# Two transformer blocks on one Trainium2 core: the first memory attention's values in PSUM banks 2 and 3, and the second memory's norm turn behind them

## What is computed

```python
# first block, memory attention: 4 heads of 128
q = rmsnorm(heads(rmsnorm(x, norm_xq) @ w_mq, 4), mq_norm)
k, v = split(rmsnorm(mem, norm_mem) @ w_mkv, 2)
k = rmsnorm(heads(k, 4), mk_norm)
p = softmax(q k^T * 128**-0.5)
x = x + (p v) @ w_mo
# second block, much later; depends on mem_2 alone, so its keys are worked on early
kv = rmsnorm(mem_2, mem_g_2) @ xa_wkv_2
```

## Time and profile before

| | |
|---|---|
| median of three runs | 1182.5 us (1180.4 to 1182.51) |
| profiled execution, first to last instruction | 1180.3 us |
| mean granted clock of PE in it | 0.996 |
| PE busy | 1152.7 us, 98% of the span |
| DVE busy | 811.4 us, 69% |
| ACT busy | 621.6 us, 53% |
| DMA, share of 16 engines | 49% for the weights' queue |

### The profile page before, as it was taken

One profiled execution on the slowest core, in us unless ns is written; L12 is line 12 of the kernel. 1 busy time (PEld: TensorE's weight loads), 2 busy tenths in 40 slices (PEclk: granted clock), 3 DMA queues, 4 the chain that ended last, 5 costly groups with the idle time before them and its releaser, 6 DMA issues.

```text
span 1180.3 us, 16847 instructions
## 1 busy us (share of the span) xinstructions
PE 1152.7 (98%) x6797; PEld 1006.6 (85%) x6797; DVE 811.4 (69%) x881; ACT 621.6 (53%) x801; POOL 87.0 (7%) x118
## 2 busy tenths in 40 slices
PE   8999999999999999999999999999999998999997
PEld 8978998888987799999888888888777887888886
DVE  6897657755878667878547777637866747777743
ACT  7666354435668556656436444436355546444432
POOL 7101101210000000000000000002700000000000
PEclk9999999999999999999999999999999999999999
DMA  8654323333665355555665556555634523665560
GB/s 257 195 160 150 111 82 107 112 103 108 214 214 179 107 170 170 166 192 185 211 204 177 183 183 201 192 182 169 211 111 149 187 93 123 198 212 178 179 213 36
DMA packets 144420, 193.95 MB, mean 164 GB/s; under 512 B 6168, under 2 KB 121240, under 8 KB 144344
## 3 DMA queue, kind: packets, MB, share of 16 engines
q1 hardware_dynamic: 143144, 188.43, 49.0%
q0 software_dynamic: 1200, 4.46, 1.1%
HBM read 191.82 MB, written 1.05 MB: 163 GB/s over the span
## 4 chain that ended last, share of the span: by engine, by line
PE 68%; DVE 8%; ACT 4%; issue 2%; DVEq 0%; ACTq 0%
PE banks L1371 19%; PE banks L1337 19%; PE banks L1319 10%; PE banks L1340 9%; DVE wlo L1925 3%; PE banks L1356 2%; PE banks L1347 1%; PE banks L1594 1%; ACT whi L1654 1%; PE banks L1385 1%; PE banks L1552 1%; PE banks L1473 1%; PE banks L1482 0%; DVE x_tok L2195 0%; PE banks L1549 0%
## 5 line engine op out<-in xcount | busy, mean ns | idle before, releaser
L1925 DVE TENSOR_TENSOR wlo<-raw,whi 128x2048 fp32r<-128x2048 f32 (+1 forms) x178 | 406.2, 2290 | 121.6 <-ACT whi L1654 121.3
L1654 ACT ACTIVATE whi<-raw 128x2048 fp32r<-128x2048 f32 (+1 forms) x179 | 340.0, 1903 | 239.8 <-PE banks L1340 137.9
L1337 PE MATMUL banks<-xhl,whi 128*128 128x512 f32 x1232 | 396.5, 403 | 2.7 <-DVE y5l L2250 1.8
L1340 PEld LDWEIGHTS banks<-xhl,wlo 128*128 128x128 f32 x1232 | 231.7, 188 | 54.2
L1340 PE MATMUL banks<-xhl,wlo 128*128 128x256 f32 x1232 | 242.9, 278 | 0.0
L1337 PEld LDWEIGHTS banks<-xhl,whi 128*128 128x128 f32 x1232 | 188.8, 189 | 9.6 <-issue 5.1
L1319 PE MATMUL banks<-xhl,whi 128*128 128x256 f32 x912 | 165.5, 285 | 1.2 <-DVE xhl L1952 0.7
L1319 PEld LDWEIGHTS banks<-xhl,whi 128*128 128x128 f32 x912 | 142.1, 192 | 2.1 <-DVE xhl L1952 1.1
L1319 PE MATMUL banks<-xhl,wlo 128*128 128x256 f32 x456 | 129.2, 283 | 0.0
L1371 PE MATMUL banks<-whi,hh 128*128 128x512 f32 x264 | 103.0, 390 | 0.0
L1371 PE MATMUL banks<-wlo,hh 128*128 128x512 f32 x264 | 102.9, 390 | 0.0
(11 more groups left out here) (370 smaller groups left out, 1549.0 us busy)
## 6 DMA issues: line engine op xcount, KB each, us to landing
raw<-in_w_in SPq DMA_DIRECT2D x40, 1024.0 KB, 5.3
raw<-in_w_up SPq DMA_DIRECT2D x22, 1024.0 KB, 5.6
raw<-in_ffn_w_gate SPq DMA_DIRECT2D x22, 1024.0 KB, 5.3
raw<-in_ffn_w_up SPq DMA_DIRECT2D x22, 1024.0 KB, 5.3
raw<-in_ffn_w_down SPq DMA_DIRECT2D x22, 1024.0 KB, 5.0
raw<-in_w_down SPq DMA_DIRECT2D x11, 1024.0 KB, 6.5
raw<-in_w_out SPq DMA_DIRECT2D x8, 1024.0 KB, 5.1
raw<-in_xa_wkv SPq DMA_DIRECT2D x8, 1024.0 KB, 5.3
```

Source lines behind the costliest of these rows:

```text
L1337: pe.matmul(bank(b[m]), wh[:, k, m * P:(m + 1) * P], both[:, k, :, :].rearrange("p a t -> p (a t)"), start=(k == 0), stop=(k == KD - 1), s ...
L1340: ins = pe.matmul(bank(b[m])[:, 0:T], wl[:, k, m * P:(m + 1) * P], Xh[:, k, :], start=False, stop=(k == KD - 1), skip_group_check=True)
L1654: act.activation(columns(whi, c, part), columns(raw, c, part), ACT.Copy).then_inc(act_done, 1)
L1925: dve.tensor_tensor(columns(wlo, c, part), columns(raw, c, part), columns(whi, c, part), ALU.subtract).then_inc(dve_done, 1)
```

## The change

The values' two chunks accumulate in banks 2 and 3 instead of 6 and 7. With that, the scores of head 1 no longer wait for ACT's copy of the values, in the plan and in the code. And the second memory's norm turn is no link of a chain any more: it stands in the plan behind the two chunks of values, before the two of `xk`.

```diff
@@ build_chunks
-    vals("w_mkv", 512, "m1", "vcopy", (6, 7), to="mv")
+    vals("w_mkv", 512, "m1", "vcopy", (2, 3), to="mv")
@@ input_of
-        if name == "sc" and args == ["mem", 1]:
-            return pl.ended.get(("copy", max(c for c, ch in enumerate(chunks) if ch.get("to") == "mv")), 1e9)
@@ build_plan
     side.append(hn("mq0", "mq1"))
-    turn_m2 = [[lambda: norm_turn("mem_g_2", 0, "m2")]]
-    side.append(turn_m2)
-    finished[id(turn_m2)] = max(pl.ended["nd", "mem_g_2", 1], pl.ended["add", c - 1])
     for lane in range(2):
         side.append(heads_of("mem", [lane, lane + 2]))
     mm(c)
     mm(c + 1)
     c += 2
-    while turn_m2:
-        place(turn_m2.pop(0)[0])
+    norm_turn("mem_g_2", 0, "m2")
     mm(c)
     mm(c + 1)
@@ sc, on PE
                 elif kind == "mem":
                     pe.wait_ge(dve_done, at("hn_mul", f"mq{h // 2}"))
-                    if h == 1:
-                        pe.wait_ge(act_done, at("copy", chunk_of("mv", None)))
```

## The result

The changed kernel takes 1185.71 us (median of 7 runs, 1184.9 to 1186.16) against 1182.5 for the kernel before (7 runs, 1180.4 to 1183.24). The ratio is 1.0032, with a 95% interval of 1.0023 to 1.0042. The forecast was 1185.0 us, a loss just beyond 0.2%.

What follows compares the result with a forecast made beforehand. PE, busy 1152.7 of 1180.3 us, was taken as the bound. Waits 5.55 + 0.6 - 1.05 - 2.55 and clock 1.4 - 1.4 gave about +2.5 us, so a median of 1185.0 us, range 1182 to some 1187.4.

Steps and rivals of the forecast that it cites:

- The order: PE, ACT and DVE queues from chunk 48 to 51: scores and exponentials of heads 0 and 1 precede the turn's high parts.
- the planned margin of 0.28: At chunk 48's end: the scores of heads 0 and 1 clear their hook by 0.28 of planned time, preceding the turn.
- the tie of 409.30 against 409.30: At the hook after half of chunk 50: lane 1 gets in with planned 409.30 against a limit of 409.30.
- the second rival: Before `w_mo`: head 1's output falls behind `lo` 52 on DVE, about 1.1 us more wait, 1186.1 us; chance 0.1.
- The turn's wait: Before chunk 49: its first matmul waits for the whole turn, leaving PE without work for 5.55 us.
- What is removed: `mq1`'s sum waiting on `mq0` (1.05 us), the wait before `w_mo` (2.55), the slow clock after it (1.4); together 5.0 us.
- The small wait: Before `w_mo`: chunk 51 waits for banks 0 and 1, emptied by chunk 50's `add`; 0.6 us, between 0 and 0.6.
- The clock behind chunk 49: Behind chunk 49's start: PE's slow level after the long wait costs 1.4 us, with bounds of 0 and 2.0.
- The sum: Whole kernel: waits 5.55 + 0.6 - 1.05 - 2.55 = +2.55, clock 1.4 - 1.4 = 0, so about +2.5 us.
- The first (no slow clock): Behind chunk 49's wait: no slow clock, or less of the small wait; +0.5, thus 1183 to 1184 us; chance 0.25.
- The third (turn ahead of the softmax): On ACT and DVE: turn precedes softmax, chunk 49 starts at 388.1, -2.5, thus 1180.0 us; chance 0.15 with all else faster.
- The range: Kernel time from 1182 to some 1187.4 us, leaving out the faster rival.

Runs made afterwards that it cites:

- the exchange: Against the changed kernel: banks of the second memory's two key chunks exchanged, chunk 49 in 0 and 1, chunk 50 in 2 and 3; 1182.57 us.
- the seventh kernel: Against the exchange: exponentials of heads 0 and 1 moved behind the turn's high part 3 on ACT, their maxima behind low part 7 on DVE; 1183.29 us.
- the kernel with the turn elsewhere: Against the kernel before: values in banks 2 and 3, turn still under chunk 48 but through 6, 7, 0, 1, key chunks' banks exchanged; 1179.31 us.
- The filler: Against the changed kernel: 40 transposes of the identity into unused bank 5, between the turn and chunk 49's waits; 1183.3 us.
- only the turn behind: Against the kernel before: only the turn moved behind the values, which stay in banks 6 and 7, with head 1's wait left in; 1190.09 us.
- the filler on top of the bank exchange: Against the exchange: 28 transposes of the identity added between the turn and chunk 49; 1182.42 us.

## Why the prediction came out right

- **The order.** PE, ACT and DVE run in the order that was derived; each row above falls in its place. The scores were let in, as the planned margin of 0.28 said, and so was head 1's product at the tie of 409.30 against 409.30, so the second rival did not come.
- **The turn's wait.** Predicted: PE out of work at 385.4, chunk 49 at 390.95, 5.55 us. Measured: 384.06 + 1.67 = 385.7 and 391.19, 5.5 us. Its two causes are shown one at a time: the banks by the exchange (5.2 to 3.5 us), the softmax ahead of the turn on ACT and DVE by the seventh kernel (3.5 to 1.7).
- **What is removed.** The waits of 1.05 and 2.55 us and the slow clock behind the second are gone from the changed kernel. That clock was priced a little low, at 1.4 us, because the count stopped at 409.61. In the kernel before the next matmul of `w_mo` follows only 0.61 us later; in the kernel with the turn elsewhere, in the same place behind a product, it follows after 0.42:

```profile
410.22 0.39 PE L1371 MATMUL banks<-wlo,y2h 128*128 128x512 f32 x1
```

```profile
407.70 0.58 PE L1371 MATMUL banks<-whi,y2h 128*128 128x512 f32 x1
408.12 0.39 PE L1371 MATMUL banks<-wlo,y2h 128*128 128x512 f32 x1
```

So the clock cost 1.6 us, and 5.2 us went in all. The kernel with the turn elsewhere bears it out for the two at `w_mo`: 2.55 + 1.6 = 4.15 us, and its stretch is 4.2 us shorter.
- **The small wait.** 0.6 us predicted; PE could have started `w_mo` at 411.15 + 0.44 = 411.6 and started at 411.94: 0.35.
- **The clock behind chunk 49: the term that was mis-sized.** It stood in the sum as 1.4 us, from the kernel before, with an upper bound of 2.0. From 391.19 to 396.45 PE did one quarter of chunk 49 (1.4 us at full clock, 388.40 to 389.79 in the kernel with the turn elsewhere), a sum (0.85) and four matmuls (0.7), 2.95 and 0.1 of start, in 5.26: 2.2 us. The filler gives 2.25 from outside. By the windows the slow level lay over PE's work from chunk 49's start to about 395.9; these are 4.7 us of dense matmuls, and half of that is 2.35. So the term was about 0.8 too small, and its bound, drawn from 3.6 us of slow work, too low.
- **The sum.** 5.5 + 0.35 + 2.2 - 5.2 = +2.85 against +2.55; the stretch shows 2.8, the spans 3.0, the medians 3.2. That the forecast came within 0.3 us of the stretch is in part luck: the clock behind chunk 49 was 0.8 too small, while 0.2 too little was taken off for the clock at `w_mo`, and the two waits together were put 0.3 too long.
- **The rivals.** The first (no slow clock) fails by the windows, in the one execution that was profiled. The third (turn ahead of the softmax) did not happen, and made real it was not faster either: its forecast of 1180.0 was wrong by almost 5 us, because the later softmax returns as a wait ahead of `w_mo`. The prediction priced that rival without following DVE to the end.
- **The range.** By its own words (1186.7 and a microsecond of spread) its upper end is 1187.7 and not 1187.4. Nothing hangs on it.
- **The rule.** "Perfetto Trace Analysis", section "Matmuls", in the Trainium skill, asks that independent groups of matmuls rotate through PSUM banks. The runs agree as far as the rule reaches: the exchange, which gives chunk 49 banks that the turn leaves earlier, is worth 2.8 us of the stretch, and sending the turn through the idle 6 and 7 makes the fastest kernel here. But chunk 49 is not independent of the turn, whose output it reads, and 3.5 us of its wait stayed with the exchange.

Two things are left open. Whether the last wait, 0.9 us of the sum of `mq1` for `hn_mul` of `mq0`, can go as well without a new one was not tried in the kernel with the turn elsewhere. And each size of the slow clock is that of one execution; how it spreads over executions at this place is not measured.

## What to carry to other kernels

Freeing a lane from a wait by moving an accumulation to other banks has a second half: what used those banks so far must go somewhere, and if it goes behind the accumulation it loses the matmuls that hid it. Look first for banks that the change itself makes idle (here 6 and 7, for the turn), and give the next accumulation the banks that are released first. When work is reordered, walk every engine's queue to the next point where PE waits; three of the reorderings here only moved the wait.

## What the runs showed of the hardware

A wait of PE in dense work can cost more than its length, and how much is not fixed. The wait for the exponentials of the third branch, 1.8 us, is the same in all kernels. These rows are of the kernel before, where the clock stays full behind it,

```profile
208.73 0.70 PE L1619 MATMUL banks<-S,sv_ 128*128 128x256 f32 x2 [1.79 <-ACT S L1844]
```

```profile
210.00:212.00 2.00, 1.70 (x11) 1.36 (x10) 0.48 (x1) 1.97 (x6) 0.00 (x0) 1.00 0.58 204
```

and these of the kernel with the turn elsewhere, whose instructions up to there are the same:

```profile
208.80 0.70 PE L1619 MATMUL banks<-S,sv_ 128*128 128x256 f32 x2 [1.80 <-ACT S L1844]
```

```profile
210.00:212.00 2.00, 2.00 (x8) 1.72 (x7) 0.55 (x1) 1.97 (x6) 0.00 (x0) 0.55 0.57 202
```

The very wait of the earlier trace rows, 1.82 us with the full clock behind it, comes 3.5 us earlier in the kernel with the turn elsewhere, and there it is followed by the slow level:

```profile
864.92 0.70 PE L1337 MATMUL banks<-xhl,whi 128*128 128x512 f32 x2 [1.81 <-DVE y5l L2250]
```

```profile
866.00:868.00 2.00, 2.00 (x9) 1.81 (x9) 2.00 (x2) 0.00 (x0) 0.00 (x0) 0.50 0.03 8
```

So the statement in the prediction that a wait of 1.82 us was not followed by the slow level told of one execution and no rule. Nor does the length decide by itself: 2.2 us before `w_mo` was followed by it in the kernel before, 2.3 us with only the turn behind and 2.1 us with the softmax behind the turn were not. "TensorE: Matmul & The Clock Gate" in the Trainium skill (Part 1) says that the monitor behind the gate does not start with the kernel, so that the number of slow matmuls varies from run to run. The executions here fit that, but show nothing of the monitor itself. Such stretches came and went at about 210, 852, 858 and 866 us, over work that no edit touched, and a comparison of medians did not tell a local gain of 1.75 us from them. The stretch between two fixed instructions of the profile did, with the filler on top of the bank exchange: 1.75 us there, 0.15 in the medians.
